# One change to a two-block transformer kernel on one core: where the relative-bias copies are written, what the expert weight stream waits for, and how the first expert's tokens are gathered

## What is computed

```python
# first block
mod = silu(c) @ w_ada + b_ada                    # six rows: shift, scale, gate of both halves
h = rmsnorm(x) * (1 + scale_m) + shift_m
proj = h @ w_in                                  # retention q k v gate, attention q k v
x = x + gate_m * rmsnorm(concat(y_ret, y_att) @ w_out)
h = rmsnorm(x) * (1 + scale_f) + shift_f
affinity = softmax(h @ w_router)                 # 16 experts, each takes its top 32 tokens
xe = h[idx]                                      # gather
ye = (silu(xe @ w_gate[e]) * (xe @ w_up[e])) @ w_down[e]   # 24 MB of weights per expert
x = x + gate_f * rmsnorm(scatter_add(ye * gates))
# two layers, each
x = x + 0.5 * swiglu_ffn(rmsnorm(x), ffn1_wi, ffn1_wo)     # D_FF 2816
... mLSTM branch and sliding-window attention with rel_bias[t5_bucket(distance)] ...
x = x + 0.5 * swiglu_ffn(...); x = x + gate * (p @ w_ple)
```

## Time and profile before

| | |
|---|---|
| median of 3 runs | 2320.9 us (2316.99 to 2321.66) |
| the profiled execution | 2319.57 us, span 2317.8 us |
| busy share of the span | PE 81%, PE weight load 55%, DVE 46%, ACT 30%, POOL 2% |
| moved by DMA | 660.83 MB, mean 285 GB/s |
| chain that ended last | PE 55%, DMA 38%, DVE 4%, ACT 2% |

### The profile page before, as it was taken

One profiled execution on the slowest core, in us unless ns is written; L12 is line 12 of the kernel. 1 busy time (PEld: TensorE's weight loads), 2 busy tenths in 40 slices (PEclk: granted clock), 3 DMA queues, 4 the chain that ended last, 5 costly groups with the idle time before them and its releaser, 6 DMA issues.

```text
span 2317.8 us, 30979 instructions
## 1 busy us (share of the span) xinstructions
PE 1886.3 (81%) x11483; PEld 1285.3 (55%) x11483; DVE 1073.8 (46%) x1500; ACT 698.0 (30%) x965; POOL 43.3 (2%) x68
## 2 busy tenths in 40 slices
PE   6896765566555556556699999999999999999999
PEld 4774311111121112111388888788878888778887
DVE  3464100000000000000388877688868887777886
ACT  4331100000000000000344456454454445544444
POOL 0000000000000000000000010000000001000000
PEclk8996977777788877777899999999999999999999
DMA  9786999999999999999755654545545575444552
GB/s 368 259 321 275 429 429 428 429 428 429 428 428 428 428 429 428 429 428 429 310 191 181 234 178 128 175 153 179 201 146 191 172 241 179 136 142 165 184 189 83
DMA packets 174820, 660.83 MB, mean 285 GB/s; under 512 B 10051, under 2 KB 108140, under 8 KB 143732
## 3 DMA queue, kind: packets, MB, share of 16 engines
q1 hardware_dynamic: 171980, 654.12, 72.9%
q10 hardware_dynamic: 2376, 3.03, 0.6%
q0 software_dynamic: 352, 2.11, 0.3%
HBM read 656.60 MB, written 2.64 MB: 284 GB/s over the span
## 4 chain that ended last, share of the span: by engine, by line
PE 55%; DMA 38%; DVE 4%; ACT 2%; issue 1%; ACTq 0%; DVEq 0%; PEldq 0%; SPq 0%; PEld 0%
PE PS L1992 26%; DMA turned_and_rows<-in_w_down_e 13%; PE PS L2080 12%; DMA turned_and_rows<-in_w_gate_e 12%; DMA turned_and_rows<-in_w_up_e 11%; PE PS L2082 6%; PE PS L1948 3%; DVE arena L210 2%; PE PS L1671 2%; DVE units L210 1%; PE PS L1968 1%; DMA ring<-in_w_in 1%; DMA ring<-in_w_ada 1%; ACT units L210 1%; PE PS L2128 1%
## 5 line engine op out<-in xcount | busy, mean ns | idle before, releaser
L210 ACT ACTIVATE units<-ring 128x1024 fp32r<-128x1024 f32 (+2 forms) x416 | 438.4, 1054 | 489.9 <-PE PS L2082 266.4
L210 DVE TENSOR_TENSOR units<-ring,units 128x1024 fp32r<-128x1024 f32 (+2 forms) x416 | 505.9, 1216 | 117.1 <-ACT units L210 82.4
L2080 PE MATMUL PS<-hT_split,units 128*128 128x512 f32 x1216 | 432.4, 398 | 0.0
L210 DVE SCALAR_TENSOR_TENSOR arena<-arena,PS 128x512 f32<-128x512 f32 (+1 forms) x54 | 41.4, 768 | 770.6 <-ACT arena L210 489.6
L210 ACT ACTIVATE arena<-PS 128x512 f32<-128x512 f32 (+3 forms) x137 | 67.7, 494 | 919.9 <-PE PS L1956 309.4
L2082 PE MATMUL PS<-hT_split,units 128*128 128x256 f32 x1216 | 341.3, 281 | 0.0
L1992 PE MATMUL PS<-units,hT_split 128*128 128x512 f32 (+2 forms) x1248 | 285.1, 386 | 4.5 <-DVE hT_split L210 2.5
L2080 PEld LDWEIGHTS PS<-hT_split,units 128*128 128x128 f32 x1216 | 228.5, 188 | 55.9
L1992 PEld LDWEIGHTS PS<-units,hT_split 128*128 128x128 f32 x1248 | 230.5, 189 | 49.2 <-issue 4.4
L1992 PE MATMUL PS<-units,hid_split 128*128 128x512 f32 x1056 | 255.4, 391 | 0.0
L2082 PEld LDWEIGHTS PS<-hT_split,units 128*128 128x128 f32 x1216 | 229.6, 189 | 3.0
(11 more groups left out here) (214 smaller groups left out, 1430.8 us busy)
## 6 DMA issues: line engine op xcount, KB each, us to landing
ring<-in_ffn_wi SPq DMA_DIRECT2D x88, 1024.0 KB, 5.5
ring<-in_w_gate_e SPq DMA_DIRECT2D x24, 2048.0 KB, 36.7
moe_ring<-in_w_up_e SPq DMA_DIRECT2D x24, 2048.0 KB, 36.2
ring<-in_w_down_e SPq DMA_DIRECT2D x24, 2048.0 KB, 35.5
moe_ring<-in_w_gate_e SPq DMA_DIRECT2D x24, 2048.0 KB, 35.9
ring<-in_w_up_e SPq DMA_DIRECT2D x24, 2048.0 KB, 35.8
moe_ring<-in_w_down_e SPq DMA_DIRECT2D x24, 2048.0 KB, 36.2
ring<-in_ffn_wo SPq DMA_DIRECT2D x44, 1024.0 KB, 5.0
```

Of the source, the lines that this page charges most:

```text
L210: return instruction(*args, **kwargs)
L2080: first = mm(PS[:, bank, :].rearrange("p (i n) -> p i n", i=2), w[0], hT_split[:, :, k, :], start=(k == 0), stop=False, skip_group_check=True)
```

## The change

Four edits, in one diff:

1. The table `rep` stays in `early` until attention's last scores. DVE then copies it to `p_rows` (`rep_kept`). The write to `skew` is no longer issued by ACT early in the first block but by SP, in layer 0, as the first transfer of `layer_constants`. The reads of `skew`, `w_ple` and `p` move into `layer_tables`, behind the net's last step.
2. `w_router` is asked for by SP, behind `w_out` (and after `ret_y`). The expert stream then waits for `mod_full` 32.
3. The copies of the weight units 16 and 17 move from between heads to behind head 2 (ACT) and behind the scores of head 3 (DVE).
4. The first gather multiplies the other way round: the one-hot of four experts is stationary and 512 columns of the rows move, so rows come out. ACT and DVE copy them to SBUF, and eight transposes bring them to the old form.

```diff
+        rep_kept = p_rows.rearrange("p t n -> p (t n)")[0:SW_H, 0:3 * P]
+        group_rows = gated.rearrange("p t e c -> p (t e c)")
...
# SP, behind the w_out fills
+            sp.wait_ge(S["ret_y"], 1)
+            sp.dma_start(w_router, a["w_router"][0].rearrange("(p k) e -> p k e", k=KT)).then_inc(S["router_full"], 16)
+            sp.wait_ge(S["mod_full"], 32)
...
                 def layer_constants():
-                    sp.wait_ge(S["skew_written"], 16)
-                    sp.dma_start(band, bass.AP(skew.tensor, P, [[3 * P - 1, P], [3 * P * P, SW_H], [1, TOK]])).then_inc(
-                        S["band_full"], 16)
+                    if l == 0:
+                        sp.wait_ge(S["rep_copied"], 2)
+                        sp.dma_start(skew.rearrange("h p n -> h p n"), rep_kept.unsqueeze(1).to_broadcast(
+                            [SW_H, P, 3 * P])).then_inc(S["skew_written"], 16)
...
+                def layer_tables():
+                    sp.wait_ge(S["skew_written"], 16)
+                    sp.dma_start(band, bass.AP(skew.tensor, P, [[3 * P - 1, P], [3 * P * P, SW_H], [1, TOK]])).then_inc(
+                        S["band_full"], 16)
                     sp.dma_start(w_ple, a["w_ple_2"][l].rearrange("(j p) n -> p j n", p=P)).then_inc(S["ple_full"], 16)
                     sp.dma_start(pT, a["p_2"][l, 0].rearrange("(j p) n -> p j n", p=P)).then_inc(S["ple_full"], 16)
...
                 ffn(POS_LAYER + OFF_FFN1, "ffn1_wi_2", "ffn1_wo_2", layer_constants)
+                layer_tables()
...
# ACT
             activation(rep, PS[0:SW_H, 6, 0:3 * P], ACT.Copy).then_inc(S["rep_copied"], 1)
-            act.wait_ge(S["rep_copied"], 1)
-            program.dma_start(skew.rearrange("h p n -> h p n"), rep.unsqueeze(1).to_broadcast([SW_H, P, 3 * P])).then_inc(
-                S["skew_written"], 16)
...
             att_copy(0)
-            first_hi(16, 17)
             att_copy(1)
...
-                    first_hi(18, 19)
+                    first_hi(16, 17, 18, 19)
...
-                if t == 0:
-                    program.dma_start(w_router, a["w_router"][0].rearrange("(p k) e -> p k e", k=KT)).then_inc(
-                        S["router_full"], 16)
...
+            act.wait_ge(S["gathered"], 1)
+            activation(group_rows[:, 0:512], PS[:, 6, :], ACT.Copy).then_inc(S["xeT"], 1)
...
# DVE
             att_scores(2)
-            first_lo(16, 17)
             att_scores(3)
-            first_lo(18, 19)
+            first_lo(16, 17, 18, 19)
...
             att_scores(7)
+            dve.wait_ge(S["rep_copied"], 1)
+            dve.run(V.tensor_copy, rep_kept, rep).then_inc(S["rep_copied"], 1)
...
+            dve.wait_ge(S["gathered"], 2)
+            dve.run(V.tensor_copy, group_rows[:, 512:D], PS[:, 7, :]).then_inc(S["xeT"], 1)
...
# PE
             for half in range(2):
-                for k in range(4):
-                    last = gather(PS[:, 6 + half, k * P:(k + 1) * P], 4 * half + k, 0, GROUP)
+                for t in range(NT):
+                    for i in range(2):
+                        last = mm(PS[:, 6 + half, :], onehot_rounded[:, t, 0:GROUP, :].rearrange("p e c -> p (e c)"),
+                                  hn_split[:, i, t, 512 * half:512 * half + 512], start=(t + i == 0), stop=(t + i == NT))
                 last.then_inc(S["gathered"], 1)
+            pe.wait_ge(S["xeT"], 2)
+            for k in range(KT):
+                last = nc.tensor.transpose(PS[:, 6 + k // 4, (k % 4) * P:(k % 4 + 1) * P], group_rows[:, k:D:KT], ident)
+                if k % 4 == 3:
+                    last.then_inc(S["gathered"], 1)
```

More of the change, by code:

```diff
@@ L801, in _ @@
             for k in range(0, KT, 2):
-                act.wait_ge(S["gathered"], 2 + k + 1)
+                act.wait_ge(S["gathered"], 4 + k + 1)
                 activation(xeT[:, k, P:NE * CAP], PS[:, LATE_BANK[k % 4], 0:NE * CAP - P], ACT.Copy).then_inc(S["xeT"], 1)
-            act.wait_ge(S["gathered"], 2 + KT + 1)
+            act.wait_ge(S["gathered"], 4 + KT + 1)
             activation(GT.rearrange("p q n -> p (q n)"), two_banks(0), ACT.Copy).then_inc(S["GT"], 1)
@@ L1247, in _ @@
                 last.then_inc(S["selected"], 1)
+            dve.wait_ge(S["gathered"], 2)
+            dve.run(V.tensor_copy, group_rows[:, 512:D], PS[:, 7, :]).then_inc(S["xeT"], 1)
             for half in range(2):
-                dve.wait_ge(S["gathered"], half + 1)
+                dve.wait_ge(S["gathered"], 2 + half + 1)
                 last = dve.run(V.tensor_copy, xe[:, 4 * half:4 * half + 4, :],
@@ L1256, in _ @@
             for k in range(1, KT, 2):
-                dve.wait_ge(S["gathered"], 2 + k + 1)
+                dve.wait_ge(S["gathered"], 4 + k + 1)
                 dve.run(V.tensor_copy, xeT[:, k, P:NE * CAP], PS[:, LATE_BANK[k % 4], 0:NE * CAP - P]).then_inc(S["xeT"], 1)
-            dve.wait_ge(S["xeT"], 1 + KT)
+            dve.wait_ge(S["xeT"], 3 + KT)
             def hidden_rows(q):
@@ L1901, in _ @@
             for half in range(2):
-                for k in range(4):
-                    last = gather(PS[:, 6 + half, k * P:(k + 1) * P], 4 * half + k, 0, GROUP)
+                for t in range(NT):
+                    for i in range(2):
+                        last = mm(PS[:, 6 + half, :], onehot_rounded[:, t, 0:GROUP, :].rearrange("p e c -> p (e c)"),
+                                  hn_split[:, i, t, 512 * half:512 * half + 512], start=(t + i == 0), stop=(t + i == NT))
                 last.then_inc(S["gathered"], 1)
+            pe.wait_ge(S["xeT"], 2)
[3 more added lines that the diff above has]
+                    last.then_inc(S["gathered"], 1)
             def gather_rest():
                 pe.wait_ge(S["selected"], 4)
-                pe.wait_ge(S["xeT"], 1)
+                pe.wait_ge(S["xeT"], 3)
                 for k in range(KT):
                     if k == 4:
-                        pe.wait_ge(S["xeT"], 1 + 4)
+                        pe.wait_ge(S["xeT"], 3 + 4)
                     gather(PS[:, LATE_BANK[k % 4], 0:NE * CAP - P], k, GROUP, NE).then_inc(S["gathered"], 1)
-                pe.wait_ge(S["xeT"], 1 + KT)
+                pe.wait_ge(S["xeT"], 3 + KT)
                 pe.wait_ge(S["selected"], 5)
```

## The result

| | kernel before | changed kernel |
|---|---|---|
| median of 7 runs each | 2318.99 us | 2325.39 us |
| lowest to highest | 2316.99 to 2321.9 | 2322.84 to 2330.04 |
| ratio after / before | | 1.0024, 95% interval 1.0015 to 1.0033 |
| the profiled execution, and its span | 2319.57, 2317.8 | 2330.04, 2328.2 |

The changed kernel is slower by 0.24%, or 5.6 us. The profiled execution after is the longest of its seven, 4.6 us over their median, so what is summed up from it comes out that much high.

The account below looks back on a forecast made before the run. The expert stage was taken as bound by its DMA stream, the two layers by PE's work. Terms -5.9 - 3.0 - 2.8 - 1.2 + 16.0 gave +3.1, forecast 2323 us, range 2308 to 2330.

Parts of the forecast that it names:

- term 5: First net, layer 0: the moved write takes 31 us, delays step 10's fills, PE stands 13.6 us and loses clock; +16.0 us.
- the clock behind head 2: Sign at head 2: a granted clock of 1.00 after PE's gap, which shrinks from 6.64 to at most 2 to 3 us.
- the wait before step 10: Sign in layer 0's first net: one PE wait of 11 to 17 us between steps 9 and 10; wrong if under 8.
- Term 1: Head 2: ACT no longer waits for unit 16's slot, PE starts `rv` 5.2 us sooner at a higher clock; -5.9 us.
- Term 2: Modulation row: its write and read run ahead of the expert stream, shortening DVE's wait; -3.0 us, bounds 0 and 4.90.
- Terms 3 and 4: Router weights asked for sooner, so PE's first logits do not wait, -2.8 us; first gather with 512-column products, -1.2 us.
- The stream: Expert stream: its end moves with the first expert's start, 12.9 us sooner; eight blocks in by 207 to 208 us.
- Rival B: Before step 10, layer 0: the write takes 35 us or more; at 37 us the term is +22, time 2330; chance 0.26.
- it belongs to the write: Cause given for the write's pace, 33 packets per us, since it held while DMA was far from full.

Follow-up runs that it names:

- e_spread: Changed kernel with the write in the same place in the net, but from 128 source partitions instead of eight; 2306.26 us, ratio 0.9933.
- f_writeonly: Kernel before with one edit alone, the eight-row write moved to SP's queue in the first net; 2331.63 us, ratio 1.0042.
- f_oldorder: e_spread with weight units 16 to 19 split where they were in the kernel before; 2302.78 us, ratio 0.9914.
- e_nomod: e_early without SP's wait for the modulation rows, so the expert stream starts ahead of them; 2313.06 us, ratio 0.9957.
- e_early: Changed kernel with the eight-row write put back in the head on ACT's queue, DVE's copy dropped; 2305.38 us, ratio 0.9942.
- e_rows: Changed kernel with the write in the same place on SP, but as eight DMAs of one head each; 2352.47 us, ratio 1.0137.

## Why the prediction was right, and where it was not

The forecast was 2323 us, with 2318 to 2328 as its own range and no measurable change as its sign. Measured were 2325.4 and +0.24%, just past the bound of 0.2%. The mechanism and the place of each term were right. Three sizes and one cause were not.

That the total came so near is in part luck. e_spread is the whole change with the write made short: -15.5 us where terms 1 to 4 forecast -12.9. The slow write is the difference from there to +5.6, that is 21.1 us where term 5 has 16.0. The two errors, 2.6 and 5.1 us, lie on opposite sides. In the profiled execution alone the terms add up to -4.6 - 4.8 - 3.1 - 1.4 + 3.6 + 20.3 = +10.0. It is the longest of seven: the four at a mean granted clock of 0.903 or 0.904 took 2322.8 to 2325.4 us, the three at 0.899 took 2326.0 to 2330.0. Where in the kernel those lose it is open.

Of the signs named ahead two were missed: the clock behind head 2 (0.76, not 1.00), and the wait before step 10, 17.57 us where at most 17 was said.

**Term 1, forecast -5.9, measured -4.6** (POOL's row write at 157.37, not 162.02). The start of `rv` was right, 98.2 forecast and 98.08 measured. Mis-sized is the clock: 1.2 us of it were to come back, but behind the wait of 2.45 us that was left the 24 products took 7.33 us, 0.4 more than before. The step that was not seen is what the reordering does: I credited the gain to ACT no longer waiting for the slow write, and took the later splitting of unit 16 as the new limit without asking what the old order would give. f_writeonly shows the write's removal alone to be worth 8.9 us at the first expert, and f_oldorder against e_spread shows the reordering to take 4.3 of that back.

**Term 2, forecast -3.0, measured -4.8** (DVE's multiplications at 166.33 without a wait, 9.4 sooner in all). I chose the middle of the bounds. Rows of after show 2.04 us from the write's issue to the read's, and e_nomod brings the 6.0 us back. The Trainium skill (DMA: Bandwidth & Descriptors, "Anatomy of one DMA — SWDGE (gpsimd) path") gave 2.0 us for the write and an estimate of 4.4 for the read, and thereby a term of -4.9. The trace has 2.04 us to the next issue and 5.1 us to the read's landing: DVE no longer waits, the term agrees within 0.1 us, and I should have followed it.

**Terms 3 and 4, forecast -2.8 and -1.2**, were in size: the first tile's logits come 12.56 us sooner, 3.1 beyond terms 1 and 2, and the gather adds 1.4. Undone alone, they are worth 2.4 and 1.4 us at the first expert. (The eight products of the gather took 3.75 us, not 3.4.)

**The stream** behaved as worked out: refill at 208.55 instead of 222.72, and the last expert product 13.4 us sooner. Not foreseen were 1.3 and 1.8 us of clock at its end. The last expert product took 3.2 to 3.6 us in every kernel with an earlier stream but 1.93 before. The wait ahead of it is no clear reason: 3 us in most of them where it was 1.57 before, but only 1.29 in e_nomod, with 3.64 us of products. The first 48 `up` products took 6.0 us in some profiles and 7.6 to 8.5 in others (e_early 6.00, e_spread 7.76, e_nomod 8.50); what decides stays open.

**Term 5, forecast +16.0, measured +20.3**, is the mis-sized one. The write's pace was right (33 forecast, 35 measured). Two things were too small. SP's small loads, which I let pass in 3 to 5 us together with the fill, are held at issue by the write: 9.94 us, then 3.7 to 4.3 for each of the next five, so that the fills are only issued at 1311.85, and with 7.7 us to landing ACT starts at 1319.58. And the clock took 2.8 us, not 2.4. Rival B, whose price was +22, described this size better.

Why the write is slow, the prediction left as "it belongs to the write". By the Trainium skill (same page, "Why a DMA increments its semaphore by 16 and not by 1") the eight rows confine it to eight engines. The shares agree (46% for eight rows, 24% for four). But that is not the price: e_rows used nearly all engines and was slower, and e_spread landed after 9.5 us. What the runs vary beside it is where the source lies: one partition at a time gave 27 GB/s, partitions 4 to 7 gave 26, partitions 0 to 7 gave 54, all 128 gave 401. A fixed pace for each row, on which I had built the expectation for e_spread, does not fit, since four rows moved no more than one. The four figures fit a limit of some 27 GB/s that neighbouring partitions share in fours; 401 would be 15 such shares. That is argued from them and not tested: no run took eight rows from partitions far apart.

## What to carry to other kernels

The broadcast write from one to eight neighbouring partitions was slow on a quarter, half or nearly all of the engines, and slowed the fills beside it even from another queue. Spread such a source over all partitions first (here one wider product), and only then ask where to put the write. When two edits aim at one wait, try each alone: here either took at least half of it away, and the one that was not needed cost 4 us. The old order of units with the spread write is the fastest version measured, 0.9914 of before (0.9898 to 0.993), and 1.1% under the changed kernel by the two ratios.

## What the runs showed of the hardware

- DRAM writes of 1536-byte pieces: 27 GB/s from one source partition at a time (18 pieces a us), 26 from four neighbouring ones (16), 54 from eight (35), 401 from 128 (261).
- DMA engines counted as busy need not be moving much: 88% share at 27 GB/s in e_rows, 46% at 54 GB/s in the changed kernel, 92% at 288 GB/s in e_spread (1276:1286).
- While the slow write ran, SP was itself held at issuing its next DMAs, even those of 4 KB and less: 9.94 and then 3.7 to 4.3 us each for five more, where the same issues took 0.3 to 0.6 us in the kernel before.
- Behind a wait of PE of 2.45 us the next 24 products took 7.33 us (granted clock 0.76 from 98 to 105 us); without it, in f_oldorder, 5.74 (1.00).
